# Attention inside a hybrid decoder step: values stationary, probabilities moving, and a new order of the units

## The chip, the cores and the metric

The kernel runs as one program on 1 core of one Trainium2 chip. The metric is device time in microseconds (us); lower is better. The engines are named as in the profile: PE (TensorE, matmuls; PEld its weight loads), DVE (VectorE), ACT (ScalarE), POOL (GpSimd) and SP (SyncE, which here only issues loads). Each engine takes its own instructions strictly in order; engines wait for each other through semaphores.

## The reference, cut to what matters

One layer over 2048 prompt tokens (and 32 sample tokens), width 1024: RMSNorm, one input projection into queries, keys, values and two recurrent branches; windowed attention (8 heads of 64, 2 key/value groups of 4 heads, window 128, with sinks and ALiBi); a gated linear recurrence (RG-LRU) beside it; an output projection with residual; a SwiGLU feed-forward with residual; a final norm.

```
# attention, per 128-query block qb, keys are block qb-1 and block qb
s = q @ k.T / 8 - slope * dist            # masked outside the window
p = exp(s - m);  p = p / (sum(p) + exp(sink - m))
out = p @ v                                # 8 heads x 64
# recurrence, per channel
a = exp(-8 r softplus(-lam));  h = a * h + sqrt(1 - a*a) * (i * x)
mix = concat([out, h * gelu(gate)]);  h1 = x + mix @ w_out + b_out
```

## The kernel before

Tokens go through in 4 blocks of 512; `Fori` runs the first three, the fourth is written out after it, because it also carries the 32 sample tokens (its products are split in two halves of 272 columns). All products are float32 made of three products with rounded high and low parts (`x_hi*w_hi`, `x_lo*w_hi`, `x_hi*w_lo`; L533 to L535), 24 matmuls of 512 columns for a 128-wide output unit. Weight units stream in: SP loads a raw unit (2 buffers), ACT writes its high part (L883), DVE its low part (L1157), PE consumes it (3 buffers).

A block has four stages: head (keys, values, queries), mixers, output projection, feed-forward. The change touches the mixers and the first output units. The mixers run eight units s = 0..7. Each unit has one projection product of a recurrent branch (`gemm`, order x0 x1 y0 x2 y1 x3 y2 y3) and a half of one 128-query attention block (4 heads): `scores(s)` on PE (L628), `softmax_1(s)` on DVE (L1253 to L1264), `exps(s)` on ACT (L961, L963), `softmax_2(s)` on DVE (sum and reciprocal, `rec`), `probs_T(s)` on PE (8 transposes, L644) with its two copies out of PSUM to `pT`, one on ACT (L968, `pTa_ready`) and one on DVE (L1277, `pTb_ready`), and `attend(s)` on PE (L661), which waits for both copies. Probabilities are not normalised; after two units DVE multiplies the 128x512 result by the reciprocals (`attn_out`, L1284), PE transposes it (`attn_T`, L670), ACT copies it and writes its high part (L998, L1001) and DVE its low part (`attn_lo`, L1345), for the output projection.

Between these the same engines carry the recurrence: `conv` (L1290 to L1297) and `evacuate` of the projection (L1170) on DVE, `gates` on PE (L677) at odd s, activations on ACT, `lru_square` (L1319, L1320), `lru_lo` (L1340), `lru_scan` (L1325, L1326, L1328), `lru_mix` (L1334, L1335) and `gelu_arg` (L1312, L1313) on DVE, `lru_root` on ACT (L986, with a table load). The order is written out by hand as three loops over s, one per engine; nothing else sets it. After unit 7, PE starts the first output units in parts (`part`), around the last attention pieces.

Semaphores that matter: `freed(u)` says that DVE has evacuated projection u; `sc_read(s)` that `softmax_1(s)` is done; `p_ready(s)` that `exps(s)` is done.

## Time and profile before

| what | value |
| --- | --- |
| median of 3 runs | 2332.38 us (2332.24 to 2334.09) |
| span of the profiled execution | 2331.0 us |
| granted clock of PE, mean of the span | 0.985 |
| PE busy | 2251.5 us, 97% |
| DVE busy | 1302.4 us, 56% |
| ACT busy | 878.1 us, 38% |

The page gives the profiled execution as its span, first to last instruction; no separate outer time is shown for it. The span lies 1.4 us under the median of the runs. Busy shares are means over stages with different limits: most of the time is projection and feed-forward products, back to back. How the mixers run, which take roughly a sixth of the time, has to be read from the timelines of that stage. In a timeline, a row is a group of like instructions; "[0.97 <-ACT a_tok L998]" is idle time before it and what ended that. In the rows, block 1 is the second of the four, and its units begin at about 622 us.

### The profile page before, as it was taken

What the parts mean: (1) busy time and instruction counts of PE and PEld (TensorE: products, weight loads), DVE (VectorE), ACT (ScalarE), POOL (GpSimd) and SP (SyncE); (2) the same over time, 40 slices, a digit from 0 to 9 for tenths busy, and PEclk for the clock granted to TensorE, in tenths of its full rate; (3) what the DMA queues carried; (4) which work ended last, traced back from release to release, by engine and by line L of the source; (5) the groups of instructions that cost most, each with busy time, mean ns of one, the idle gap of its engine ahead of it and who ended that gap; (6) DMA issues with size and microseconds to landing.
All of it is one profiled execution on the core that took longest, in us unless ns stands there. A gap on an engine that the chain in (4) does not pass through costs nothing.

```text
span 2331.0 us, 31209 instructions
## 1 busy us (share of the span) xinstructions
PE 2251.5 (97%) x12165; PEld 1915.8 (82%) x12165; DVE 1302.4 (56%) x2146; ACT 878.1 (38%) x1349; POOL 32.4 (1%) x66
## 2 busy tenths in 40 slices
PE   6999999999999999999999999999999899999996
PEld 6777888888777888888877788888888799999996
DVE  4786535356587544445668653545668665444453
ACT  4574223235375322223457432323446532222221
POOL 1000000000000000000000000000000000000000
PEclk9999999999999999999999999999999899999998
DMA  4123232323313233332322323233231122222221
GB/s 148 55 68 114 91 100 90 101 89 92 101 46 118 91 97 93 92 98 92 107 67 63 119 91 98 91 97 94 92 124 45 30 91 86 87 91 82 92 80 60
DMA packets 58586, 207.34 MB, mean 89 GB/s; under 512 B 7341, under 2 KB 7549, under 8 KB 58416
## 3 DMA queue, kind: packets, MB, share of 16 engines
q1 hardware_dynamic: 51840, 184.57, 25.5%
q0 software_dynamic: 3936, 12.03, 1.5%
q10 hardware_dynamic: 2656, 8.62, 1.0%
q8 instruction: 104, 1.70, 0.3%
q14 instruction: 50, 0.41, 0.1%
HBM read 196.44 MB, written 9.77 MB: 88 GB/s over the span
## 4 chain that ended last, share of the span: by engine, by line
PE 84%; DVE 9%; ACT 4%; issue 2%; DMA 1%; ACTq 0%; DVEq 0%; POOL 0%
PE bank L533 27%; PE bank L535 27%; PE bank L534 27%; DVE s_p L1258 2%; DVE w_lo L1157 1%; DVE xc L1297 1%; PE bank L661 1%; ACT s_p L961 1%; DVE om L1326 1%; PE bank L628 1%; DVE pT L1277 1%; PE bank L583 1%; ACT L986 0%; PE bank L557 0%; DVE ii L1325 0%
## 5 line engine op out<-in xcount | busy, mean ns | idle before, releaser
L533 PE MATMUL bank<-x_hi,w_hi 128*128 128x512 f32 (+1 forms) x2320 | 826.4, 356 | 3.7 <-DVE x_lo L1187 2.6
L535 PE MATMUL bank<-x_hi,w_lo 128*128 128x512 f32 (+1 forms) x2320 | 820.3, 354 | 0.0
L534 PE MATMUL bank<-x_lo,w_hi 128*128 128x512 f32 (+1 forms) x2320 | 819.5, 353 | 0.0
L883 ACT ACTIVATE w_hi<-w_raw 128x1024 fp32r<-128x1024 f32 (+1 forms) x360 | 374.1, 1040 | 1175.3 <-PE bank L535 1175.3
L533 PEld LDWEIGHTS bank<-x_hi,w_hi 128*128 128x128 f32 x2320 | 438.9, 189 | 79.8 <-issue 13.6
L1157 DVE TENSOR_TENSOR w_lo<-w_raw,w_hi 128x1024 fp32r<-128x1024 f32 (+1 forms) x360 | 431.8, 1200 | 127.7 <-ACT w_hi L883 125.9
L534 PEld LDWEIGHTS bank<-x_lo,w_hi 128*128 128x128 f32 x2320 | 439.1, 189 | 61.8 <-issue 1.4
L535 PEld LDWEIGHTS bank<-x_hi,w_lo 128*128 128x128 f32 x2320 | 438.3, 189 | 60.8
L533 PE MATMUL bank<-a_hi,w_hi 128*128 128x512 f32 (+1 forms) x1200 | 427.4, 356 | 6.2 <-DVE a_lo L1561 1.8
L535 PE MATMUL bank<-a_hi,w_lo 128*128 128x512 f32 (+1 forms) x1200 | 425.0, 354 | 0.0
L534 PE MATMUL bank<-a_lo,w_hi 128*128 128x512 f32 (+1 forms) x1200 | 424.3, 354 | 0.0
L533 PEld LDWEIGHTS bank<-a_hi,w_hi 128*128 128x128 f32 x1200 | 227.6, 190 | 40.6 <-DVE a_lo L1345 3.2
L535 PEld LDWEIGHTS bank<-a_hi,w_lo 128*128 128x128 f32 x1200 | 227.3, 189 | 31.3
L534 PEld LDWEIGHTS bank<-a_lo,w_hi 128*128 128x128 f32 x1200 | 227.7, 190 | 30.5
L1563 DVE TENSOR_TENSOR hT<-bank,hT 128x512 f32<-128x512 f32 (+1 forms) x120 | 70.9, 591 | 235.5 <-PE bank L535 235.3
L1170 DVE TENSOR_TENSOR a<-bank,rinv 128x512 f32<-128x512 f32 (+1 forms) x110 | 65.1, 591 | 229.4 <-PE bank L535 227.6
L1170 DVE TENSOR_TENSOR gt<-bank,rinv 128x512 f32<-128x512 f32 (+1 forms) x110 | 65.0, 591 | 206.4 <-PE bank L535 206.0
L961 ACT ACTIVATE s_p<-s_p,nm 128x256 f32<-128x256 f32 x128 | 63.6, 498 | 51.5 <-DVE sd L1264 51.5
L661 PE MATMUL bank<-v_tok,pT 128*128 128x64 f32 x512 | 63.2, 278 | 8.3 <-ACT a_tok L998 8.3
L661 PEld LDWEIGHTS bank<-v_tok,pT 128*128 128x128 f32 x512 | 61.9, 197 | 10.8 <-issue 10.4
L1102 ACT ACTIVATE a_hi<-a 128x512 fp32r<-128x512 f32 (+1 forms) x88 | 56.3, 639 | 37.0 <-DVE a L1557 35.0
L1557 DVE SCALAR_TENSOR_TENSOR a<-gt,a 128x512 f32<-128x512 f32 (+1 forms) x88 | 61.7, 701 | 3.0
(240 smaller groups left out, 1475.0 us busy)
## 6 DMA issues: line engine op xcount, KB each, us to landing
w_raw<-in_units SPq DMA_DIRECT2D x296, 512.0 KB, 3.5
w_raw<-in_units SPq DMA_DIRECT2D x64, 448.0 KB, 3.3
x_tok<-in_x_prompt POOLq DMA_DIRECT2D x16, 512.0 KB, 6.1
out_y_p<-y_tok ACTq DMA_DIRECT2D x16, 512.0 KB, 3.0
gfin<-in_g_fin POOLq DMA_DIRECT2D x1, 512.0 KB, 7.1
kc_tok<-in_cache_k POOLq DMA_DIRECT2D x1, 512.0 KB, 6.9
vc_tok<-in_cache_v POOLq DMA_DIRECT2D x1, 512.0 KB, 7.3
out_nk_s<-in_cache_k POOLq DMA_DIRECT2D x1, 496.0 KB, 6.5
```

The costliest lines, as they stand in the source:

```text
L533: nc.tensor.matmul(out, h, hi[:, kt, c0:c1], start=(first and kt == kts[0]), stop=False)
L534: nc.tensor.matmul(out, h, lo[:, kt, c0:c1], start=False, stop=False)
L535: mm = nc.tensor.matmul(out, l, hi[:, kt, c0:c1], start=False, stop=(kt == kt_of[u] - 1))
L661: mm = nc.tensor.matmul(V[:, head * HEAD:(head + 1) * HEAD], pT[:, s % 2, 2 * hh + half, :], v_tok[:, qb + half, g * HEAD:(g + 1) * HEAD], ...
L883: w_hi_ready.by(A(w_hi[:, u % RING, 0:n], w_raw[:, u % RAW, 0:n], ACT.Copy))
L961: A(s_p[:, s % 2, hh, :], s_p[:, s % 2, hh, :], ACT.Exp, bias=nm[:, s % 2, hh:hh + 1], accum_out=rs[:, s % 2, hh:hh + 1])
L1102: act_hi.by(A(a_hi[:, f, 0:w], a32[:, n % 2, 0:w], ACT.Copy))
L1157: w_ready.by(TT(w_lo[:, u % RING, 0:n], w_raw[:, u % RAW, 0:n], w_hi[:, u % RING, 0:n], ALU.subtract))
L1170: return lambda src, c0, c1: TT(dst(c0, c1), src, rinv[:, c0:c1], ALU.mult)
L1258: ins = nc.vector.tensor_tensor_reduce(s_p[:, s % 2, hh, :], S[g][:, jj * 256:(jj + 1) * 256], d[:, :], 2.0 ** -(head + 1), sinks[:, head: ...
L1557: act_f.by(STT(out=a32[:, n % 2, 0:w], in0=gt[:, 0:w], scalar=0.5, in1=a32[:, n % 2, 0:w], op0=ALU.mult, op1=ALU.mult))
L1563: evacuate(b, last, u, lambda src, c0, c1: TT(hT[:, m, c0:c1], src, hT[:, m, c0:c1], ALU.add))
```

## The change

1. `attend`: before, the stationary operand is a 128x128 block of transposed probabilities and 64 columns of values move (8 matmuls, float32 runs each in two passes). Now 64 columns of values are stationary, and the probabilities of two heads (256 columns) move: 4 matmuls, alternating between group 0 (output partitions 0 to 63) and group 1 (64 to 127). The result comes out already transposed.
2. `attn_T` goes. The reciprocals now have to stand in every partition of a head's half: `spread` makes 8 matmuls with a reciprocal column broadcast to 64 columns as the stationary operand and the identity moving. ACT copies that to `a_tok` (`attn_recs`), DVE multiplies the result by it (`attn_out`, same size as before).
3. In that layout, tile c of the mixed vector holds head c of both groups, so the rows of the output weights are permuted: each of the 8 output units of a block is loaded with 5 transfers (one of 256 KB, four of 64 KB with runs of 512 bytes) in place of one of 512 KB. The sample tokens' result is written to the same layout.
4. Order on PE: `probs_T(s-1)` moves from the start of unit s to behind its `gemm`; `scores(s)` comes first, then `attend(s-2)`, `spread`; `gates` moves from behind the `gemm` into its middle. On ACT `probs_T(s-1)` moves behind the work on the evacuated projection, `lru_gates` ahead of it. On DVE the copy `probs_T(s-1)` moves from the start of unit s to behind `evacuate(s)`, and `lru_scan` ahead of `evacuate`. The last pieces after unit 7 are reordered alike.

Vector engine, even unit 4, before. `es`, `rec`: softmax_2; `w_lo`: weight split; `yb`: the evacuation; `ii`, `om`, `h_prev`: the scan; `gl`: gelu_arg; `pT`: the copy.

```order
L1270 TENSOR_TENSOR es<-es,rs 128x4 [waits p_ready]
L1272 RECIPROCAL rec<-es 128x2x2 [waits dve_chain]
L68 REGISTER_ALU [waits dve_chain]
L1157 TENSOR_TENSOR w_lo<-w_raw,w_hi 128x1024 [waits w_hi_ready]
L1170 TENSOR_TENSOR yb<-bank,rinv 128x512 [waits gemm_done]
L1325 TENSOR_TENSOR ii<-ii,qq 128x512 [waits lru_sqrt]
L1326 SCALAR_TENSOR_TENSOR om<-ra,h_prev,ii 128x512 [waits dve_chain]
L1328 COPY h_prev<-om 128x1 [waits dve_chain]
L1312 TENSOR_SCALAR gl<-gl 128x512 [waits gelu_sq,dve_chain]
L1313 SCALAR_TENSOR_TENSOR gl<-yb,vec,gl 128x512 [waits dve_chain]
L1277 COPY pT<-bank 128x512 [waits av_done,pT_done]
```

Here the copy `pT` is that of unit 4, the first instruction of unit 5's list. The same place now:

```order
L1305 TENSOR_TENSOR es<-es,rs 128x4 [waits p_ready]
L1307 RECIPROCAL rec<-es 128x2x2 [waits dve_chain]
L68 REGISTER_ALU [waits rec_ready]
L1192 TENSOR_TENSOR w_lo<-w_raw,w_hi 128x1024 [waits w_hi_ready]
L1358 TENSOR_TENSOR ii<-ii,qq 128x512 [waits lru_sqrt]
L1359 SCALAR_TENSOR_TENSOR om<-ra,h_prev,ii 128x512 [waits dve_chain]
L1361 COPY h_prev<-om 128x1 [waits dve_chain]
L1205 TENSOR_TENSOR yb<-bank,rinv 128x512 [waits gemm_done,dve_chain]
L1313 COPY pT<-bank 128x512 [waits av_done,pT_done]
L1345 TENSOR_SCALAR gl<-gl 128x512 [waits gelu_sq]
L1346 SCALAR_TENSOR_TENSOR gl<-yb,vec,gl 128x512 [waits dve_chain]
```

The scan stands ahead of the evacuation, and the copy `pT`, now that of unit 3, right behind it.

PE, ahead of the product of unit 5, before (L644 probs_T, L661 attend, L628 scores).

```order
L644 MATMUL bank<-ident,s_p 128x128 [waits pTb_ready,pTa_ready,p_ready]
L644 MATMUL bank<-ident,s_p 128x128 x7
L661 MATMUL bank<-v_tok,pT 128x64 [waits pTb_ready,pTa_ready]
L661 MATMUL bank<-v_tok,pT 128x64 x7
L628 MATMUL bank<-kT,qT 128x256 [waits sc_read]
L628 MATMUL bank<-kT,qT 128x256 x3
```

The same place now (L660 probs_T, L642 scores, L678 attend, L692 spread).

```order
L660 MATMUL bank<-ident,s_p 128x128 [waits pTb_ready,pTa_ready,p_ready]
L660 MATMUL bank<-ident,s_p 128x128 x7
L68 REGISTER_ALU
L642 MATMUL bank<-kT,qT 128x256 [waits sc_read]
L642 MATMUL bank<-kT,qT 128x256 x3
L678 MATMUL bank<-pT,v_tok 64x256 [waits pTb_ready,pTa_ready]
L678 MATMUL bank<-pT,v_tok 64x256 x3
L692 MATMUL bank<-ident,rec 64x128 [waits rec_ready]
L692 MATMUL bank<-ident,rec 64x128 x7
```

Before, the piece runs from `probs_T(4)` to `scores(5)`, and its attend is `attend(3)`. Now the transposes are `probs_T(3)`, behind the product of unit 4, and the attend is `attend(3)` too, of the copies that these very transposes are read into.

```diff
+                raw, src, landed = w_raw[:, u % RAW, :], units[u % NU], raw_in[u % RAW]
+                if u % NU not in U_O:
+                    landed.by(sp.dma_start(raw[:, 0:n], src[:, 0:n]))
+                    return
+
+                landed.by(sp.dma_start(raw[:, JT * P:n], src[:, JT * P:n]))
+                for g in range(NKV):
+                    for c in range(2):
+                        k = 2 * g + c
+                        landed.by(sp.dma_start(
+                            raw[g * HEAD:(g + 1) * HEAD, 2 * c * P:2 * (c + 1) * P].rearrange("d (o m) -> d o m", o=2),
+                            src[:, k * P:(k + 1) * P].rearrange("(o d) m -> d o m", o=2)))
...
-                        attn_moved.wait(pe, b, qb)
-                    for hh in range(HH):
-                        g, jj = hh // 2, hh % 2
-                        head = g * JT + 2 * jp + jj
-                        for half in range(2):
-                            mm = nc.tensor.matmul(V[:, head * HEAD:(head + 1) * HEAD],
-                                                  pT[:, s % 2, 2 * hh + half, :],
-                                                  v_tok[:, qb + half, g * HEAD:(g + 1) * HEAD],
-                                                  start=(half == 0), stop=(half == 1))
+                        atok_ready.wait(pe, b, qb)
+                    for half in range(2):
+                        for g in range(NKV):
+                            d = slice(g * HEAD, (g + 1) * HEAD)
+                            mm = nc.tensor.matmul(V[d, 2 * jp * P:2 * (jp + 1) * P], v_tok[:, qb + half, d],
+                                                  pT[:, s % 2, 4 * g + half:4 * g + half + 3:2, :],
+                                                  start=(half == 0), stop=(half == 1), skip_group_check=True)
                     av_done.by(mm)
 
-                def attn_T(qb):
-                    atok_ready.wait(pe, b, qb + 1)
-                    for c in range(4):
-                        mm = nc.tensor.transpose(V[:, c * P:(c + 1) * P], a_tok[:, c * P:(c + 1) * P], ident[:, :])
-                    attnT_done.by(mm)
+                def spread(qb):
+
+
+                    rec_ready.wait(pe, b, 2 * qb + 2)
+                    if last and qb == QB - 2:
+                        pe.wait_ge(smp_dve, SMP_DVE_AT)
+                    for j in range(JT):
+                        for g in range(NKV):
+                            head = g * JT + j
+                            mm = nc.tensor.matmul(TB[0][g * HEAD:(g + 1) * HEAD, j * P:(j + 1) * P],
+                                                  rec[:, qb % 2, head:head + 1].to_broadcast([P, HEAD]), ident[:, :],
+                                                  start=True, stop=True, skip_group_check=True)
+                    recs_done.by(mm)
...
+                def attn_recs(qb):
+                    recs_done.wait(act, b, qb + 1)
+                    amix_ready.wait(act, b, qb)
+                    recs_read.by(A(a_tok[:, :], TB[0][:, :], ACT.Copy))
+
                 def attn_hi(qb):
-                    attnT_done.wait(act, b, qb + 1)
-                    attn_moved.by(A(a_tok[:, :], V[:, :], ACT.Copy))
-
-                    attn_moved.wait(act, b, qb + 1)
+                    atok_ready.wait(act, b, qb + 1)
...
                 def attn_out(qb):
-                    av_done.wait(dve, b, 2 * qb + 2)
-                    amix_ready.wait(dve, b, qb)
-                    bc = rec[:, qb % 2, :].rearrange("p (h o) -> p h o", o=1).to_broadcast([P, NH, HEAD])
-                    atok_ready.by(TT(a_tok[:, :].rearrange("p (h d) -> p h d", h=NH),
-                                     V[:, :].rearrange("p (h d) -> p h d", h=NH), bc, ALU.mult))
+                    recs_read.wait(dve, b, qb + 1)
+                    atok_ready.by(TT(a_tok[:, :], V[:, :], a_tok[:, :], ALU.mult))
...
+                    scores(s)
+                    if s >= 2:
+                        attend(s - 2)
+                    if s >= 3 and s % 2 == 1:
+                        spread((s - 3) // 2)
+                    if last:
+                        gemm(b, last, UH + s, x_hi, x_lo, None, None, 0)
+                    else:
+                        gemm(b, last, UH + s, x_hi, x_lo, None, list(range(KT // 2)))
+                    if s % 2 == 1:
+                        gates(s // 2)
+                    if last:
+                        gemm(b, last, UH + s, x_hi, x_lo, None, None, 1)
+                    else:
+                        gemm(b, last, UH + s, x_hi, x_lo, None, list(range(KT // 2, KT)))
                     if s >= 1:
                         probs_T(s - 1)
-                    if s >= 2:
-                        attend(s - 2)
-                    scores(s)
-                    gemm(b, last, UH + s, x_hi, x_lo)
                     if last:
                         for step in sample_at.get(s, ()):
                             step(b, s)
-                    if s % 2 == 1:
-                        gates(s // 2)
-                    if s >= 3 and s % 2 == 1:
-                        attn_T((s - 3) // 2)
...
+                part(0, early)
+                attend(NUN - 2)
                 probs_T(NUN - 1)
-                attend(NUN - 2)
-                part(0, early)
+                part(1, early)
                 attend(NUN - 1)
-                part(1, early)
-                attn_T(QB - 1)
+                spread(QB - 1)
...
                 for s in range(NUN):
-                    if s >= 1:
-                        probs_T(s - 1)
+                    if s >= 3 and s % 2 == 1:
+                        attn_recs((s - 3) // 2)
                     exps(s)
                     if s >= 2 and s % 2 == 0:
                         lru_root((s - 2) // 2)
+                    if s >= 3 and s % 2 == 1:
+                        attn_hi((s - 3) // 2)
+                    if s % 2 == 1:
+                        lru_gates(s // 2)
                     kind, c = ORDER[s]
                     u = UH + s
                     freed.wait(act, b, u + 1)
...
 
                         lmix_ready.wait(act, b, c - 1)
                         gelu_sq.by(A(gl[:, c % 2, :], yb[:, c % 2, 0:T], ACT.Square, bias=v(VB + u)))
-                        if c < LC - 1:
-                            gelu_tanh(c)
-                    if s >= 3 and s % 2 == 1:
-                        attn_hi((s - 3) // 2)
-                    if s % 2 == 1:
-                        lru_gates(s // 2)
+                    if s >= 1:
+                        probs_T(s - 1)
+                    if kind == "y" and c < LC - 1:
+                        gelu_tanh(c)
...
                 for s in range(NUN):
-                    if s >= 1:
-                        probs_T(s - 1)
                     softmax_1(s)
+                    if s >= 3 and s % 2 == 1:
+                        attn_out((s - 3) // 2)
                     if s >= 2 and s % 2 == 0:
                         lru_square((s - 2) // 2)
                     if s >= 4 and s % 2 == 0:
...
                         sample_conv()
                     if last and s == 7:
                         sample_square()
-                    if s >= 3 and s % 2 == 1:
-                        attn_out((s - 3) // 2)
                     if s >= 1:
                         split(b, UH + s - 1 + RING)
                     if s >= 3 and s % 2 == 1:
                         lru_mix((s - 3) // 2)
+                    if s >= 2 and s % 2 == 0:
+                        lru_scan((s - 2) // 2)
                     kind, c = ORDER[s]
                     if kind == "x":
                         evacuate(b, last, UH + s, scaled(
                             lambda c0, c1: xb[:, c % 2, CONV_W - 1 + c0:CONV_W - 1 + c1]))
                     else:
                         evacuate(b, last, UH + s, scaled(lambda c0, c1: yb[:, c % 2, c0:c1]))
+                    if s >= 1:
+                        probs_T(s - 1)
                     if last and s in sample_at:
                         sample_at[s]()
                     if s >= 3 and s % 2 == 1:
                         attn_lo((s - 3) // 2)
                     if kind == "x":
                         conv(c)
-                    if s == NUN - 1:
-                        probs_T(s)
-                    if s >= 2 and s % 2 == 0:
-                        lru_scan((s - 2) // 2)
```

## Rows read from the trace of the kernel before

**Rows 1.** Timeline of PE, units 5 and 6 of block 1; columns: start us, us, what.

```profile
676.74 1.09 PE L644 MATMUL bank<-ident,s_p 128*128 128x128 f32 x8 [0.57 <-ACT es L963]
677.67 1.90 PE L661 MATMUL bank<-v_tok,pT 128*128 128x64 f32 x16
679.49 1.14 PE L628 MATMUL bank<-kT,qT 64*128 64x256 f32 x8
680.56 0.50 PE L533 MATMUL bank<-x_hi,w_hi 128*128 128x512 f32 x1
...
686.24 1.88 PE L677 MATMUL bank<-xc,gates_w 128*128 128x512 f32 x4
687.96 0.60 PE L670 MATMUL bank<-ident,a_tok 128*128 128x128 f32 x4
688.40 1.04 PE L644 MATMUL bank<-ident,s_p 128*128 128x128 f32 x8
690.40 1.97 PE L661 MATMUL bank<-v_tok,pT 128*128 128x64 f32 x16 [0.97 <-ACT a_tok L998]
```

**Rows 2.** Timeline of DVE over units 4 and 5 of the same block.

```profile
671.62 0.68 DVE L1277 COPY pT<-bank 128x512 f32<-128x512 f32 x1
...
674.42 0.69 DVE L1319 SCALAR_TENSOR_TENSOR ii<-ii,xc 128x512 f32<-128x512 f32 x1
...
676.23 0.16 DVE L1270 TENSOR_TENSOR es<-es,rs 128x4 f32<-128x4 f32 x1
...
676.72 1.23 DVE L1157 TENSOR_TENSOR w_lo<-w_raw,w_hi 128x1024 fp32r<-128x1024 f32 x1
677.86 0.68 DVE L1170 TENSOR_TENSOR yb<-bank,rinv 128x512 f32<-128x512 f32 x1
678.66 0.69 DVE L1325 TENSOR_TENSOR ii<-ii,qq 128x512 f32<-128x512 f32 x1
...
680.89 0.43 DVE L1312 TENSOR_SCALAR gl<-gl 128x512 f32<-128x512 f32 x1
...
682.02 0.68 DVE L1277 COPY pT<-bank 128x512 f32<-128x512 f32 x1
...
688.33 0.68 DVE L1170 TENSOR_TENSOR xb<-bank,rinv 128x512 f32<-128x512 f32 x1
690.95 0.69 DVE L1345 TENSOR_TENSOR a_lo<-a_tok,a_hi 128x512 fp32r<-128x512 f32 x1 [1.94 <-ACT a_hi L1001]
...
694.66 0.68 DVE L1277 COPY pT<-bank 128x512 f32<-128x512 f32 x1
```

**Rows 3.** Timeline of ACT in unit 4 of the same block.

```profile
674.51 0.51 ACT L961 ACTIVATE s_p<-s_p,nm 128x256 f32<-128x256 f32 x1 [1.16 <-DVE sd L1264]
...
676.70 1.28 ACT L986 ACT_TABLE_LOAD   x1
...
678.58 0.72 ACT L1019 ACTIVATE gl<-yb,vec 128x512 f32<-128x512 f32 x1
```

**Rows 4.** Timeline of PE, first unit of the same block.

```profile
625.92 2.08 PE L628 MATMUL bank<-kT,qT 64*128 64x256 f32 x6 [3.67 <-issue]
627.92 0.79 PE L533 MATMUL bank<-x_hi,w_hi 128*128 128x512 f32 x1
...
634.76 1.04 PE L644 MATMUL bank<-ident,s_p 128*128 128x128 f32 x8
```

**Rows 5.** One stretch around it: busy us and instructions by engine, PEclk, DMA.

```profile
623.70:630.53 6.83, 4.61 (x12) 3.29 (x12) 2.10 (x11) 1.42 (x2) 0.00 (x0) 0.50 0.18 69
```

**Rows 6.** Timeline of PE, sample attention of the last block.

```profile
1811.21 1.10 PE L786 MATMUL bank<-pcT,vc_tok 128*64 128x16 f32 x16
```

**Rows 7.** DMA issues of the page: KB each, median us to landing.

```profile
w_raw<-in_units SPq DMA_DIRECT2D x296, 512.0 KB, 3.5
...
x_tok<-in_x_prompt POOLq DMA_DIRECT2D x16, 512.0 KB, 6.1
...
kc_tok<-in_cache_k POOLq DMA_DIRECT2D x1, 512.0 KB, 6.9
```

More of the change, by code:

```diff
@@ L282, in sem @@
             return ctx.enter_context(nc.semaphore(name))
-        raw_in = [Signal(sem(f"raw_in{i}"), NU // RAW, 16) for i in range(RAW)]
+        transfers = [1 + NKV * 2 if u in U_O else 1 for u in range(NU)]
+        raw_count = [sum(transfers[u % RAW:u + 1:RAW]) for u in range(NU)]
+        raw_in = [Signal(sem(f"raw_in{i}"), sum(transfers[i::RAW]), 16) for i in range(RAW)]
         w_hi_ready = Signal(sem("w_hi_ready"), NU)
@@ L500, in smp_by, with gemm @@
                 ins.then_inc(smp_pe, 1)
-            def gemm(b, wide, u, hi, lo, tile_ready=None, kts=None, only=None):
-                whole = list(range(kt_of[u]))
-                kts = kts or whole
-                first = kts[0] == (KT - LC if kts != whole else 0)
+            def gemm(b, wide, u, hi, lo, tile_ready=None, kts=None, only=None, begins=0):
+                kts = kts or list(range(kt_of[u]))
+                first = kts[0] == begins
                 final = kts[-1] == kt_of[u] - 1
@@ L879, in split @@
                     return
-                raw_in[u % RAW].wait(act, b, u // RAW + 1)
+                raw_in[u % RAW].wait(act, b, raw_count[u % NU] + u // NU * sum(transfers[u % RAW::RAW]))
                 unit_done(act, b, u - RING)
@@ L1040, in mixers @@
                 lru_hi(LC - 2)
+                attn_recs(QB - 1)
                 lru_decay(LC - 1)
@@ L1370, in mixers @@
                         lru_mix((s - 3) // 2)
+                    if s >= 2 and s % 2 == 0:
+                        lru_scan((s - 2) // 2)
                     kind, c = ORDER[s]
@@ L1391, in mixers @@
                 softmax_2(NUN - 1)
+                probs_T(NUN - 1)
                 lru_lo(LC - 2)
```

23 lines of the change are left out of this document (12 added, 11 removed).

## The prediction

> **What bounds the kernel now.** I read the page first: PE is busy nearly all the span, so what PE does less would seem to be won, and where PE waits it would be lost. Then the timelines of the mixers, the only stage the change touches at length, engine by engine, over a pair of units (an even y unit and an odd x unit), since the pattern repeats by pairs. The reader is to see there that PE is not what sets the pace. From one copy `pT` of unit 3 to that of unit 5, two units later, DVE takes 694.66 - 671.62 = 23.04 us [rows 2], and in that time it waits once for long, 1.94 us, for ACT's `a_hi`. PE waits twice in a pair, 0.57 us for the exponentials and 0.97 us for `a_tok` [rows 1]. So both engines are within two microseconds of full, DVE is the one whose list closes the loop, and PE is let go by it. What decides the change is therefore how tightly the two lists hang together, more than the length of either.
>
> **PE's work, part by part.** `attend` takes 679.49 - 677.67 = 1.82 us for 16 passes, `probs_T` 0.93, `scores` 680.56 - 679.49 = 1.07, a product 686.24 - 680.56 = 5.68, `gates` 687.96 - 686.24 = 1.72, `attn_T` 0.44 [rows 1]. `gates` is 4 passes of 512 columns, so a pass costs 0.43 us per 512 columns, 0.21 per 256, 0.11 per 128. The new `attend` has 8 passes of 256 columns, the new `spread` 16 of 128: each 1.72 us if the passes run one after the other, 0.86 if the two groups run at the same time. No row has two matmuls side by side in column halves. The nearest is `scores`: it too has 8 passes of 256 columns, in two row halves of 64, and takes 1.07 where one after the other would be 1.72; the two halves run together, with 0.21 left for the passage between shapes. The sample's attention has 64-column weights, 16 passes in 1.03 to 1.10 us [rows 6], 0.07 each, so loading such weights doesn't bound either. I take 1.05 for `attend` and 0.95 for `spread`; the other end is 1.8 and 1.8. A pair of units then has 2 x 1.05 + 0.95 = 3.0 us where it had 2 x 1.82 + 0.44 = 4.1: 1.1 us less (or 1.3 more).
>
> The Trainium skill (TensorEngine Tiling, Key Properties) says that different tiles of the array load and multiply in parallel, and that a change of tiling mode drains the engine. By it the side-by-side value holds; the drains are the 0.21 us in `scores`, and the trace agrees as far as row halves show it. No run here shows column halves yet.
>
> **The new loop.** DVE's work stays as it was: the multiplication has the same size. Its order doesn't. Before, the copies of `probs_T(s-1)` stood at the start of DVE's unit s, so `attend` found them made long ago. Now `attend(s-2)` in PE's unit s needs the copies of `probs_T(s-2)`, which DVE makes in unit s-1 behind `evacuate(s-1)`, and the product of unit s stands behind that `attend`. So PE can't start a product before DVE has evacuated the last one and copied, and DVE can't evacuate before the product is done. They alternate. Follow a pair, from DVE's start of the evacuation of an odd unit.
>
> DVE's half: 0.9 until PE's transposes are complete; copy and `softmax_1` 674.42 - 671.62 = 2.80; between them `attn_lo` and `conv` 694.66 - 690.95 = 3.71 (the 1.94 wait is gone, since `a_hi` is now made earlier). From the end of `softmax_1` the scan waits for ACT: exponentials 676.70 - 674.51 = 2.19, then table load and root, together 678.66 - 674.42 = 4.24 [rows 2, 3]. DVE's own work in that time (`lru_square`, `lru_lo`, `softmax_2` and the split) is over at 677.86 - 674.42 = 3.44, so 0.8 is waited; before, the evacuation filled it. The scan is 680.89 - 678.66 = 2.23, then the evacuation 0.69. The copy on DVE would take 0.68, but ACT's half of it now stands behind `gelu_sq`, 0.66 + 0.58 (`gelu_sq` is 0.72 with some overlap; the size of ACT's copy I take a little under DVE's), and 0.15 of hops: 1.4. Sum 0.9 + 2.8 + 3.7 + 4.24 + 2.23 + 0.69 + 1.4 = 15.9 us. PE, meanwhile, does transposes, scores, attend, product, transposes and scores, 0.9 + 1.07 + 1.05 + 5.68 + 0.93 + 1.07 = 10.7, and then stands 5.2 us in front of `attend` of the odd unit.
>
> PE's half: attend 1.05, `spread` 0.95, product 5.68, `gates` 1.72, end of the pipeline and hop 0.2: 9.6 us. DVE has 688.33 - 682.02 = 6.3 us of work in that time and then waits about 2.6 for the product.
>
> A pair is 15.9 + 9.6 = 25.5 us against 23.04: 2.4 slower, although PE has less to do. Three pairs in a block (the loop closes at units 2, 4 and 6 into 3, 5 and 7): 7.3.
>
> At the ends of the stage. `gates(0)` now stands in the middle of product 1 and waits for `softmax_1(1)`, which DVE does behind evacuation, ACT's bias and `conv`: 0.69 + 0.72 + 3.1 + 2.2, about 6.9 with hops after product 0, where PE is there after scores and half a product, 1.07 + 2.84 = 3.9. It waits 3.0, of which less `attend` work and the rest of the product behind it give some back: +1.3. Behind unit 7, `spread(3)`, ACT's copy, ACT's decay and tanh (four instructions of the size of its 0.72, which stand before `a_hi`; about 2.8 us), `a_hi` and `a_lo` are a chain of about 6 us behind `attend(7)`, covered by 1.4 us of the third output unit and what PE does itself; PE waits some 3.5 before the late parts, nearly all of it new: +3.5. Per block 7.3 + 1.3 + 3.5 = 12, three blocks 36. In the last block a product is longer (two halves of 272 columns), which was on the path before as after, and the sample steps now stand behind `probs_T` and three of them wait for its copies: 12 + 4 = 16. Sum so far: 52.
>
> **The clock.** PE stood 3.67 us before block 1's first scores, and then 6 passes of `scores` took 2.0 us (627.92 - 625.92) where 6 of 8 passes are 0.8, and the product took 634.76 - 627.92 = 6.84 where it is 5.68 [rows 1, 4]: 2.4 us lost. In that stretch the granted clock was 0.50, that is 1.2 in place of 2.4 GHz [rows 5]; PE had been idle before it fell. The new order has five stands of over 3 us in a block (three of 5.2, the `gates` one, the last one), each followed by work that lies on the path. At 2.4 each that would be 12 a block; at nothing, 0. A part of a low stretch may lie inside the stand itself, and shorter stands do not always bring it, so I take 7: 28 us over four blocks.
>
> **Costs taken at nothing.** The five transfers for an output unit: a raw buffer is free from one split to the next but one, two products of 5.68 us less the two splits (twice the 1.14 of [rows 2]), 9 us, and a unit lands in 3.5; 512 KB in runs of 512 bytes (`kc_tok`) landed in 6.9 where whole rows of 4 KB (`x_tok`) took 6.1 [rows 7], both on POOL's queue. So I expect under 6 us, covered; uncovered it would cost 32 units times the excess, per two units. DVE's multiplication and ACT's copy are as big as before. The rearranged sample copies are as many.
>
> **Sum.** 2331.0 + 52 + 28 = 2411 for the profiled span; the median of runs stands 1.4 above the span, so about 2412.
>
> **Rivals.**
> - The same loop, but PE's clock stays up after the stands: 2331 + 52 + 1.4 = 2384 us. For it: no stand in the mixers of 5 us exists in the trace to judge by. Against: the row at 0.50.
> - The column halves don't run together: `attend` 1.8 and `spread` 1.8 add 1.6 to PE's half of each pair and some 2 at the tail, 7 a block, so 2412 + 28 = 2440. For it: no row with column halves. Against: `scores`.
> - The five transfers are slow: if each took 3.5 us one after another, 17.5 + 2.3 = 19.8 us for two units in place of 11.4, 4.2 us a unit, 32 units: about 2412 + 134 = 2546. Against it: the 512-byte row.
> - Faster: the loop doesn't close, because `attend` finds its copies early. Then PE's two waits go, and DVE's 1.94, and a pair is 23.04 - 1.9 = 21.1 us, DVE's bare work; 12 pairs give 23 us, 2309. It decides where DVE's half is shorter than PE's way to `attend`, 10.7; I find 15.9, so 5 us of error in one place would be needed. For it: PE truly has 1.1 us less per pair, and both waits of [rows 1] truly go.
> - The gains and the loop cancel: within 0.2%.
>
> **Chances.** Forecast 0.52; clock stays up 0.17; one after the other 0.18; transfers 0.03; faster 0.07; cancels 0.03. Within 0.2% (4.7 us) is what a measurement here can't tell from no change. Faster by more 0.07, same 0.03, slower 0.90. The likeliest is 2412. The range goes from 2365, below the clock case because the last block and the ends are worked out loosely, to 2450, above the serial one.
>
> **What would show it.** Right: on PE, idle of 4 to 6 us before `attend` in units 3, 5 and 7, released by a `pT` copy of ACT; on DVE a wait for the product of 2 to 3 us at the odd evacuations; a pair of 25 to 28 us; no wait on `a_tok`; `attend` 1.0 to 1.1 us and `spread` about 0.95; PEclk of 0.5 in several stretches of each mixers stage; product times in feed-forward and head unchanged. Wrong: `attend` without idle before it, or the pair at 21 us (the loop as I drew it isn't there); `attend` at 1.8 (no side by side); idle before output products ended by a load.

## The result, and the profile after

| | before | after |
| --- | --- | --- |
| median, us (4 runs each, same chip) | 2332.31 (2331.34 to 2334.09) | 2408.41 (2406.77 to 2409.41) |
| ratio, 95% interval | | 1.0324 [1.0309, 1.0339] |
| span of the profiled execution, us | 2331.0 | 2407.7 |
| mean granted clock of PE | 0.985 | 0.967 |

Slower by 76 us; 2412 was predicted. On the page PE has more busy time than before, although its matmuls in the mixers became shorter, and its share fell from 97% to 94%. A low clock makes busy time longer, so that number alone would mislead.

```profile
PE 2261.5 (94%) x12101; PEld 1897.0 (79%) x12101; DVE 1305.6 (54%) x2146; ACT 878.9 (37%) x1349; POOL 32.5 (1%) x66
```

The timeline of PE after, block 1, its gates(0), units 3 to 7 and the first late parts (start us, us, what). It answers to [rows 1, 4].

```profile
657.82 3.78 PE L701 MATMUL bank<-xc,gates_w 128*128 128x512 f32 x4 [2.92 <-DVE sd L1299]
...
665.22 1.04 PE L660 MATMUL bank<-ident,s_p 128*128 128x128 f32 x8
...
680.86 1.97 PE L678 MATMUL bank<-pT,v_tok 128*64 128x256 f32 x8 [4.65 <-ACT pT L998]
...
693.90 1.08 PE L678 MATMUL bank<-pT,v_tok 128*64 128x256 f32 x8
...
700.58 1.03 PE L660 MATMUL bank<-ident,s_p 128*128 128x128 f32 x8
...
707.75 1.98 PE L678 MATMUL bank<-pT,v_tok 128*64 128x256 f32 x8 [5.06 <-ACT pT L998]
709.51 1.92 PE L692 MATMUL bank<-ident,rec 128*64 128x128 f32 x16
...
714.28 1.88 PE L701 MATMUL bank<-xc,gates_w 128*128 128x512 f32 x4
...
734.80 1.97 PE L678 MATMUL bank<-pT,v_tok 128*64 128x256 f32 x8 [5.05 <-ACT pT L998]
...
754.41 0.50 PE L547 MATMUL bank<-a_hi,w_hi 128*128 128x512 f32 x1 [0.74 <-DVE w_lo L1192]
...
758.52 0.50 PE L547 MATMUL bank<-a_hi,w_hi 128*128 128x512 f32 x1 [1.75 <-DVE a_lo L1378]
```

To read there: PE stands 4.65 to 5.06 us in front of `attend` (L678) of the odd units, and what ends the stand is ACT's copy `pT`. In the even units (693.90) it doesn't stand at all. A pair of units, from odd `attend` to odd `attend`, takes 707.75 - 680.86 = 26.89 and 734.80 - 707.75 = 27.05 us, where it had 23.04 [rows 2]. Right behind a stand `attend` is busy for 1.98 us, elsewhere for 1.08.

The other side of the loop, in the timeline of DVE after; it answers to [rows 2].

```profile
703.53 0.69 DVE L1358 TENSOR_TENSOR ii<-ii,qq 128x512 f32<-128x512 f32 x1 [0.71 <-ACT qq L1016]
...
705.76 0.69 DVE L1205 TENSOR_TENSOR yb<-bank,rinv 128x512 f32<-128x512 f32 x1
...
718.97 0.69 DVE L1205 TENSOR_TENSOR xb<-bank,rinv 128x512 f32<-128x512 f32 x1 [3.15 <-PE bank L549]
```

And of ACT, which makes the other half of the copy.

```profile
706.49 0.72 ACT L1055 ACTIVATE gl<-yb,vec 128x512 f32<-128x512 f32 x1 [2.99 <-DVE yb L1205]
707.12 0.58 ACT L998 ACTIVATE pT<-bank 128x512 f32<-128x512 f32 x1
```

The product that `yb` evacuates ended about where the transposes behind it begin, at 700.58, but DVE comes to it at 705.76: the scan, which waits for ACT's root `qq`, stands ahead. Only then come evacuation, `gelu_sq`, ACT's copy (ends 707.70) and `attend` (707.75). In the other half DVE waits 3.15 us for PE. The engines take turns.

The stage by windows, block 1 from its first scores to its first late part, one stretch around a stand, and one in the last block (stretch, length, busy us and instructions of PE, PEld, DVE, ACT and POOL, PEclk, DMA). First before:

```profile
625.92:722.54 96.62, 92.77 (x500) 72.79 (x499) 77.09 (x194) 67.19 (x142) 0.00 (x0) 0.98 0.14 45
```

Then after:

```profile
641.73:758.52 116.79, 96.39 (x484) 69.07 (x483) 78.07 (x194) 68.62 (x142) 0.00 (x0) 0.88 0.12 36
704.60:711.40 6.80, 3.65 (x25) 2.56 (x25) 5.62 (x17) 4.07 (x5) 0.00 (x0) 0.50 0.17 52
1885.60:1906.10 20.50, 14.32 (x85) 11.67 (x86) 7.68 (x28) 8.16 (x22) 0.00 (x0) 0.50 0.09 27
```

The stage is 116.79 - 96.62 = 20.2 us longer. Its idle time went from 3.9 to 20.4 us. From 704.60 to 711.40, around a stand, the granted clock was 0.50, that is 1.2 GHz; PE had been idle before. The last stretch belongs to the last block and is read below.

Where in the block the 20.2 lie is read against three rows of PE in before:

```profile
655.06 1.90 PE L661 MATMUL bank<-v_tok,pT 128*128 128x64 f32 x16
...
700.70 1.90 PE L661 MATMUL bank<-v_tok,pT 128*128 128x64 f32 x16
...
1729.86 1.14 PE L628 MATMUL bank<-kT,qT 64*128 64x256 f32 x8 [1.42 <-ACT qT L948]
```

Up to the `attend` of unit 3: 680.86 - 641.73 = 39.1 against 655.06 - 625.92 = 29.1, +10.0 (the stand of gates(0) and the first stand before `attend`). The next two pairs: 53.94 against 45.64, +8.3. From there to the late part: 23.7 against 21.8, +1.9. Over the program: block 1 begins 641.73 - 625.92 = 15.8 later, the scores of the last block 1786.00 - 1729.86 = 56.1 later (row below), so blocks 1 and 2 together cost 40.3; the last one and what follows cost 76.7 - 56.1 = 20.6.

The last block shows that the same total can come from other places. PE after:

```profile
1786.00 1.14 PE L642 MATMUL bank<-kT,qT 64*128 64x256 f32 x8 [1.41 <-ACT qT L978]
...
1826.85 1.97 PE L678 MATMUL bank<-pT,v_tok 128*64 128x256 f32 x8 [4.68 <-ACT pT L998]
...
1857.47 1.97 PE L678 MATMUL bank<-pT,v_tok 128*64 128x256 f32 x8
...
1889.75 1.86 PE L816 MATMUL bank<-pcT,vc_tok 128*64 128x16 f32 x16 [8.71 <-ACT pT L998]
...
1902.25 1.97 PE L678 MATMUL bank<-pT,v_tok 128*64 128x256 f32 x8
```

Here only unit 3 has the stand before `attend`. In units 5 and 7 (1857.47 and 1902.25) PE waits ahead of the scores instead, 2.89 and 2.03 us, both for sample work, and `attend` behind them still takes 1.97 us. The sample attention (L816) waits 8.71 us for an ACT copy, and from 1885.60 to 1906.10, 20.5 us on end, the granted clock is 0.50 (the window above).

### The profile page after: what moved, and what is told of

It is laid out like the page before. It is cut to its first block, busy times and chain, and to the rows that moved or that the text cites. A ratio compares the mean times of both kernels' runs of the same rounds, so it can differ in the third digit from the quotient of the medians.

```text
span 2407.7 us, 31226 instructions
## 1 busy us (share of the span) xinstructions
PE 2261.5 (94%) x12101; PEld 1897.0 (79%) x12101; DVE 1305.6 (54%) x2146; ACT 878.9 (37%) x1349; POOL 32.5 (1%) x66
## 4 chain that ended last, share of the span: by engine, by line
PE 86%; DVE 7%; ACT 4%; issue 2%; DMA 1%; ACTq 0%; POOL 0%; DVEq 0%
PE bank L547 26%; PE bank L549 26%; PE bank L548 26%; PE bank L701 1%; PE bank L678 1%; DVE s_p L1293 1%; DVE xc L1330 1%; PE bank L692 1%; ACT s_p L991 1%; DVE om L1359 1%; ACT L1016 1%; PE bank L660 1%; PE bank L597 1%; PE bank L571 0%; PE bank L642 0%
## 5 line engine op out<-in xcount | busy, mean ns | idle before, releaser
L547 PE MATMUL bank<-x_hi,w_hi 128*128 128x512 f32 (+1 forms) x2320 | 834.8, 360 | 3.1 <-DVE x_lo L1222 1.9
L678 PE MATMUL bank<-pT,v_tok 128*64 128x256 f32 x256 | 45.4, 487 | 52.0 <-ACT pT L998 49.0
L678 PEld LDWEIGHTS bank<-pT,v_tok 128*64 128x64 f32 x256 | 19.1, 166 | 71.9 <-ACT pT L998 60.2
```

The lines of the kernel that those rows point to most:

```text
L547: nc.tensor.matmul(out, h, hi[:, kt, c0:c1], start=(first and kt == kts[0]), stop=False)
L678: mm = nc.tensor.matmul(V[d, 2 * jp * P:2 * (jp + 1) * P], v_tok[:, qb + half, d], pT[:, s % 2, 4 * g + half:4 * g + half + 3:2, :], start ...
```

## The experiments

Each edit is to the changed kernel, unless it says otherwise. Times are medians; each ratio is against the kernel before, run on the same chip.

**e1_scan_back** moves one call on DVE, the scan, back behind the evacuation and the copy.

```diff
-                    if s >= 2 and s % 2 == 0:
-                        lru_scan((s - 2) // 2)
                     kind, c = ORDER[s]
...
                     if kind == "x":
                         conv(c)
+                    if s >= 2 and s % 2 == 0:
+                        lru_scan((s - 2) // 2)
```

> The changed kernel with one part undone: DVE's scan stands behind the evacuation and the copy of the probabilities again, as before the change. Theory A (DVE and PE alternate, and DVE's half is lengthened by the scan's wait for ACT's root and by the scan): the way from the end of softmax_1 to the even evacuation falls from 4.24 + 2.23 us to 3.44, so PE's stand before attend of the odd units falls from 5 us to about 2, and a pair of units from 27.0 us to 22.5 (24 if the clock still falls behind the stand). Twelve pairs: 2408 - 36 to - 54, so 2354 to 2372 us. Rival B (the stands come from PE's own new work or from the output units' transfers): no change, 2408.

Measured 2365.7 us (2364.89 to 2367.79), ratio 1.0146 [1.0129, 1.0163]: 43 of the 76 us are back by one call. PE in its timeline:

```profile
647.11 3.78 PE L701 MATMUL bank<-xc,gates_w 128*128 128x512 f32 x4 [2.92 <-DVE sd L1299]
...
689.26 1.08 PE L678 MATMUL bank<-pT,v_tok 128*64 128x256 f32 x8 [2.00 <-ACT pT L998]
690.17 1.04 PE L692 MATMUL bank<-ident,rec 128*64 128x128 f32 x16
...
711.73 1.08 PE L678 MATMUL bank<-pT,v_tok 128*64 128x256 f32 x8 [2.00 <-ACT pT L998]
```

The pair is 711.73 - 689.26 = 22.47 us, the stand 2.00 in place of 5.06, and `attend` is 1.08 behind it: the clock did not fall there. The gates(0) stand of 2.92 with its slow 3.78 is unchanged. So the pairs hang on what stands between the product's end and DVE's evacuation.

**e2_copy_first** puts ACT's copy ahead of its work on the evacuated product (`gelu_sq` or the bias).

```diff
                         lru_gates(s // 2)
+                    if s >= 1:
+                        probs_T(s - 1)
                     kind, c = ORDER[s]
...
-                    if s >= 1:
-                        probs_T(s - 1)
                     if kind == "y" and c < LC - 1:
```

> The changed kernel with ACT's copy of the probabilities ahead of its work on the evacuated projection (in an even unit ahead of gelu_sq). Theory A: ACT's copy is what ends PE's stand; with it early DVE's own copy ends it, 0.6 us sooner in each odd unit, 12 times: about 2401 us, and the stand is released by DVE. Rival B (another wait sets the pair): within 0.1% of 2408.

Measured 2406.97 us (2406.47 to 2408.83), ratio 1.0323 [1.0306, 1.0340]: no gain, against the expectation.

```profile
708.49 1.98 PE L678 MATMUL bank<-pT,v_tok 128*64 128x256 f32 x8 [4.69 <-DVE pT L1313]
...
735.71 1.97 PE L678 MATMUL bank<-pT,v_tok 128*64 128x256 f32 x8 [4.69 <-DVE pT L1313]
```

The stand is 0.37 us shorter and DVE's copy now ends it, as expected, but the pair is 735.71 - 708.49 = 27.22 us, not shorter. A window around the first of these rows shows where the gain went:

```profile
706.90:713.70 6.80, 5.21 (x28) 3.99 (x29) 5.46 (x19) 5.07 (x10) 0.00 (x0) 0.50 0.10 27
```

The stretch at 0.50 is as long here as in after (704.60 to 711.40 above), but it begins 1.6 us before `attend` and not 3.2. So PE works 5.21 us of it at the low clock, where after works 3.65. From `attend` to `gates` it then takes 715.70 - 708.49 = 7.21 us, where after takes 714.28 - 707.75 = 6.53. Why the stretch begins later in the stand isn't shown.

**e3_filled** has PE work in its stand: 18 (in the last block 30 narrower) matmuls whose result is thrown away.

```diff
                 for s in range(NUN):
                     scores(s)
+                    if s >= 3 and s % 2 == 1:
+                        fill(s, 18 if not last else 30)
                     if s >= 2:
```

> The changed kernel with added work: ahead of attend in units 3, 5 and 7 PE runs 18 more matmuls of 512 columns (30 of 272 in the last block) into the bank that the next product overwrites; nobody reads them. They take 4.2 us of a stand of 5. Theory A (the clock falls because PE stands, and costs 1.4 us in each pair): the granted clock stays at 1.0 behind the filled stands, attend takes 1.0 us instead of 1.8, a pair 25.6 instead of 27.0, and the kernel gets faster by about 17 us, 2391, though it does more. Rival B (attend, spread and the first product are slow behind a stand for a reason other than the clock, or the added work delays attend): 2408 or more.

Measured 2396.02 us (2393.22 to 2398.39), ratio 1.0269 [1.0252, 1.0287]: 12 us faster with more work. PE's rows:

```profile
701.08 1.08 PE L678 MATMUL bank<-pT,v_tok 128*64 128x256 f32 x8 [0.72 <-ACT pT L1013]
...
705.87 1.88 PE L701 MATMUL bank<-xc,gates_w 128*128 128x512 f32 x4
...
726.39 1.08 PE L678 MATMUL bank<-pT,v_tok 128*64 128x256 f32 x8 [0.72 <-ACT pT L1013]
...
1769.24 1.14 PE L642 MATMUL bank<-kT,qT 64*128 64x256 f32 x8 [1.41 <-ACT qT L993]
...
1839.19 5.09 PE L715 MATMUL bank<-x_hi,w_hi 128*128 128x272 f32 x30
1844.21 1.08 PE L678 MATMUL bank<-pT,v_tok 128*64 128x256 f32 x8
```

and the stage of block 1, from first scores to first late part as before:

```profile
637.22:748.26 111.04, 103.65 (x537) 75.19 (x537) 78.05 (x194) 68.06 (x142) 0.00 (x0) 0.96 0.13 39
```

The loop still takes turns, but at 2.4 GHz (0.96 over the stage, where after has 0.88): the pair is 726.39 - 701.08 = 25.31 us. From `attend` to `gates` it takes 705.87 - 701.08 = 4.79 us, where after takes 6.53. So one such stand costs 1.74 us through the clock, beside its own length. The gain fell short of the 17 expected in one place: the scores of the last block come 1786.00 - 1769.24 = 16.8 us earlier, and then 5.7 are lost again (the two profiled executions differ by 11.1). Two of the three odd units of that block, 5 and 7, have no stand before `attend` to fill. There the added work lies on the path: 1844.21 - 1839.19 = 5.0 us in unit 5, as much in unit 7, of which the clock gives back some 2 each.

**e4_one_transfer** loads each output unit in one transfer.

```diff
-        transfers = [1 + NKV * 2 if u in U_O else 1 for u in range(NU)]
+        transfers = [1 for u in range(NU)]
...
-                if u % NU not in U_O:
+                if True:
                     landed.by(sp.dma_start(raw[:, 0:n], src[:, 0:n]))
```

> The changed kernel with each output unit loaded by one transfer of 512 KB as before the change; the rows of the output weights are then left in the old order, so the output projection multiplies the wrong heads. Theory A (the five transfers are covered): within 0.1% of 2408. Rival B (a wait for the splits of an output unit is longer for them; one of 0.74 us stands ahead of the third output unit): faster by up to 4 x 0.7 = 3 us or more.

Measured 2408.0 us (2406.21 to 2410.21), ratio 1.0322 [1.0305, 1.0339]: the five transfers cost nothing that can be measured.

**e5_scan_gates_back** is e1 and, besides, `gates` behind the whole product on PE, with ACT's part behind the bias.

```diff
                         gemm(b, last, UH + s, x_hi, x_lo, None, list(range(KT // 2)))
-                    if s % 2 == 1:
-                        gates(s // 2)
...
                         gemm(b, last, UH + s, x_hi, x_lo, None, list(range(KT // 2, KT)))
+                    if s % 2 == 1:
+                        gates(s // 2)
```

> Two parts of the order undone: the scan behind the evacuation (as in e1_scan_back, 2366 us) and the gates' matmuls behind the whole product again, with ACT's gates behind the bias. Theory A (in the middle of product 1 they wait 2.9 us for softmax_1(1) and drag the clock down behind it; elsewhere their place is indifferent, because the copies of the probabilities wait for the transposes behind both): no stand at gates(0), no low clock there, the other pairs stay at 22.5 us; 3 us a block, about 2354 us. Rival B (the middle place hides gates and is a gain in the later units): slower than 2366.

Measured 2350.47 us (2347.3 to 2352.47), ratio 1.0076 [1.0060, 1.0093]: 15 us less than e1, 3.8 a block. The place of `gates` (on PE, with ACT's part) was the second cost. `gates(0)` starts at 642.46 without idle before it, and from the first scores of block 1 to the `attend` of unit 3 it takes 657.41 - 625.63 = 31.8 us, where e1 takes 667.02 - 630.73 = 36.3. Part of these 4.5 us is lost again, for the expectation missed something: PE now waits some 2 us before the scores of even units. PE, unit 4 of block 1, and the same unit one block later:

```profile
669.72 1.14 PE L642 MATMUL bank<-kT,qT 64*128 64x256 f32 x8 [1.98 <-ACT ii L1005]
670.79 1.08 PE L678 MATMUL bank<-pT,v_tok 128*64 128x256 f32 x8
...
1225.42 1.53 PE L642 MATMUL bank<-kT,qT 64*128 64x256 f32 x8 [1.98 <-ACT ii L1005]
1226.88 1.97 PE L678 MATMUL bank<-pT,v_tok 128*64 128x256 f32 x8
```

The same wait of 1.98 us has the full clock behind it once and the low one the other time. Where the clock stays up a pair takes 679.70 - 657.41 = 22.3 us; in the next block, where it falls, 1236.94 - 1213.12 = 23.8.

**e6_old_order** keeps the new matmuls and gives all three engines the old order, as far as the new operations allow.

```diff
                 for s in range(NUN):
+                    if s >= 1:
+                        probs_T(s - 1)
                     scores(s)
                     if s >= 2:
                         attend(s - 2)
-                    if s >= 3 and s % 2 == 1:
-                        spread((s - 3) // 2)
...
-                    if s % 2 == 1:
-                        gates(s // 2)
+                    if s >= 3 and s % 2 == 1:
+                        spread((s - 3) // 2)
...
-                    if s >= 1:
-                        probs_T(s - 1)
...
+                    if s % 2 == 1:
+                        gates(s // 2)
```

DVE and ACT likewise: `probs_T(s - 1)` at the start of the unit, `lru_scan` behind the evacuation.

> The new matmuls in the old order: attend with values stationary, spread and the five transfers of the changed kernel, but transposes and copies of the probabilities at the start of a unit as before, gates behind the product, the scan behind the evacuation; spread stands in the middle of the odd products, ACT copies its result ahead of the bias, DVE multiplies behind the evacuation and writes a_lo behind conv. Theory A (all of the loss is the order; the new matmuls themselves save PE 1.1 us a pair and take a_tok's copy off attend's path): PE waits under 1 us anywhere, a pair 22 us against 23.04 of the kernel before, about 3 us a block: 2319 us (2312 to 2326). Rival B (DVE's list alone bounds the stage, so the matmuls are worth nothing): 2331. Rival C (the new matmuls or transfers cost): over 2335.

Measured 2324.36 us (2321.26 to 2324.69), ratio 0.9963 [0.9949, 0.9977]: faster than before. Run again as e10 it gave 2322.54 and 0.9964 [0.9950, 0.9977]. PE:

```profile
663.57 1.14 PE L642 MATMUL bank<-kT,qT 64*128 64x256 f32 x8 [0.76 <-ACT ii L1007]
664.64 1.08 PE L678 MATMUL bank<-pT,v_tok 128*64 128x256 f32 x8
...
678.17 1.09 PE L693 MATMUL bank<-ident,rec 128*64 128x128 f32 x16 [0.74 <-ACT pT L1000]
...
686.68 1.08 PE L678 MATMUL bank<-pT,v_tok 128*64 128x256 f32 x8
```

The pair is 686.68 - 664.64 = 22.04 us, 1.0 below before, as the 1.1 us less work on PE would have it (the two waits of a pair, 0.76 and 0.74, add up to what the 0.57 and 0.97 of before did). `attend` waits for nothing; two waits of about 0.75 us remain, at the scores of the even unit and at `spread` (L693), which stands in the middle of the product and needs the bank that ACT's copy frees.

**e7_group_by_group** issues the four matmuls of `attend` in the order group 0, 0, 1, 1 in place of 0, 1, 0, 1.

```diff
-                    for half in range(2):
-                        for g in range(NKV):
+                    for g in range(NKV):
+                        for half in range(2):
```

> The changed kernel with attend's four matmuls issued group by group (0, 0, 1, 1) in place of alternating. Theory A (the two column halves run at the same time as the row halves of scores do, which are issued group by group): attend stays at 1.0 to 1.1 us, 2408. Rival B (only neighbours in the list overlap): attend takes 1.3 to 1.8 us, a pair up to 0.8 us longer in its PE half, up to 2418.

Measured 2407.75 us (2405.64 to 2408.99), ratio 1.0324 [1.0307, 1.0342]. The row for all of L678 in this kernel, minimum, median and maximum of one pass in ns:

```profile
L678 PE MATMUL bank<-pT,v_tok x256: 379/430/689, 95.2 to 1917.5; 128*64 128x256 f32 x128
```

After has 379/430/688: no difference. That two passes run side by side, and not merely fast, is seen in the starts of the single passes, which the timeline gathers into one row. In e1's `attend` at 689.26 the eight begin at 689.261 and 689.267, 689.527 and 689.534, 689.743 and 689.750, 689.959 and 689.966; in e7 the two of a pair are 13 to 14 ns apart. That it takes both halves shows in the sample attention of before, whose 64-column weights all lie in one half (`TB[g][0:HEAD]`): there no two of a group's 16 passes begin together; after the first they follow each other by 58 to 59 ns.

So with four passes of a group in a row (e7) the halves still overlap. With many in a row they don't, as far as row halves show it. The sample scores of after issue 16 passes of one group (and two of another matmul) before the other group's:

```profile
L793 PE MATMUL bank<-kc_T,q_d x32: 272/272/373, 1848.7 to 1852.1; 64*128 64x128 f32 x32
```

32 passes of 128 columns in 3.4 us are 0.11 each, one after the other; only where the groups meet do two begin together (1850.367 and 1850.373). For long runs of one group the order of issue may well matter; no run tests it for column halves.

**e8_scan_back_copy_first** is e1 and e2 at once: is e2's edit worth something when the clock stays up?

```diff
+                    if s >= 1:
+                        probs_T(s - 1)
                     kind, c = ORDER[s]
...
+                    if s >= 2 and s % 2 == 0:
+                        lru_scan((s - 2) // 2)
```

> e1_scan_back (2366 us) with ACT's copy ahead of its other work too. Theory A (in e2_copy_first the stand got 0.4 us shorter, but spread and product behind it lost as much to the low clock; behind the 2 us stands of e1_scan_back the clock does not fall, so here the same edit is worth what it takes off): a pair 22.0 instead of 22.5, 12 times: about 2360 us. Rival B (the edit is worth nothing in itself): 2366.

Measured 2360.25 us (2356.89 to 2364.89), ratio 1.0116 [1.0099, 1.0132], against 1.0146 [1.0129, 1.0163] for e1: the intervals touch, so a gain of some 5 us is likely and not shown. PE:

```profile
687.71 1.08 PE L678 MATMUL bank<-pT,v_tok 128*64 128x256 f32 x8 [1.66 <-DVE pT L1313]
...
693.14 1.98 PE L701 MATMUL bank<-xc,gates_w 128*128 128x512 f32 x4 [0.49 <-DVE sd L1299]
...
710.23 1.08 PE L678 MATMUL bank<-pT,v_tok 128*64 128x256 f32 x8 [1.65 <-DVE pT L1313]
```

The stand is 0.34 us shorter than in e1, but the pair, 710.23 - 687.71 = 22.52, is not: `gates` then waits 0.49 us for `softmax_1` on DVE. The time came near the number expected of the theory that the edit helps when the clock stays up; the mechanism did not show, at least in the profiled execution (2364.89, the slowest of the four). The pair is set by DVE's list there, not by ACT's copy.

**e9_spread_late** is e6 with its two remaining waits attacked: `spread` behind 6 of the 8 parts of the product, and in even units `attend` ahead of `scores`.

The diff is to e6.

```diff
+                    if s >= 2 and s % 2 == 0:
+                        attend(s - 2)
                     scores(s)
-                    if s >= 2:
+                    if s >= 3 and s % 2 == 1:
                         attend(s - 2)
...
-                        gemm(b, last, UH + s, x_hi, x_lo, None, list(range(KT // 2)))
+                        gemm(b, last, UH + s, x_hi, x_lo, None, list(range(KT - 2)))
                     if s >= 3 and s % 2 == 1:
                         spread((s - 3) // 2)
```

> e6_old_order with two places changed on PE, except in the last block for the first: spread stands behind six of the eight parts of the odd product instead of four (there it waited 0.7 us for ACT's copy of the probabilities), and in even units attend stands ahead of scores (which waited 0.8 us for ACT's gates). Theory A (PE's two waits set part of the pair): both waits vanish, a pair 22.0 to 21.4 us, 9 to 12 pairs, 6 us: 2318. Rival B (DVE's list sets the pair at 22.0): PE waits elsewhere, 2324 again.

Measured 2313.28 us (2312.52 to 2316.82), ratio 0.9926 [0.9912, 0.9940], beside 0.9964 for e10, run on the same chip. It is the fastest version. PE:

```profile
660.59 1.08 PE L678 MATMUL bank<-pT,v_tok 128*64 128x256 f32 x8
662.17 1.14 PE L642 MATMUL bank<-kT,qT 64*128 64x256 f32 x8 [0.50 <-ACT ii L1009]
...
676.77 1.09 PE L693 MATMUL bank<-ident,rec 128*64 128x128 f32 x16
...
681.97 1.08 PE L678 MATMUL bank<-pT,v_tok 128*64 128x256 f32 x8
```

`spread` waits no longer, the scores wait 0.50, and the pair is 681.97 - 660.59 = 21.38 us. Only PE's order differs from e6 here, so the rival that DVE's list sets the pair at 22.0 falls.

**e10_old_order_again** is e6 once more, unchanged, to see that its small gain stands.

> e6_old_order once more, beside e9_spread_late on the same chip and in more rounds. If the gain over the kernel before is real: ratio 0.9965 within 0.0015, about 2324 us. If it was the chip's scatter: the interval holds 1.

It does: 2322.54 us (2321.28 to 2325.34).

## Why the prediction was right

The step that decided held: the two lists alternate. Point by point.

- **What set the pace before.** The prediction took it that DVE's list closes the loop and lets PE go. e6 and e9 don't bear that out as it stands. With less work on PE the pair fell from 23.04 to 22.04 us (e6), and with PE's order alone changed to 21.38 (e9), so PE's list had a part in the 23.04. The forecast of the change didn't rest on this.
- **The loop.** Predicted: PE's half, DVE's half, a pair of 25.5 us without the clock. With the clock kept up (e3) it is 25.31. DVE's half, from the odd evacuation to the end of ACT's copy, was worked out as 15.9 and is 15.8 (734.80 - 718.97, from the evacuation to the `attend` that it lets go). The stand before `attend` was to be 5.2 and is 4.65 to 5.06, ended by the ACT copy named; DVE's wait at the odd evacuation was put at 2.6 (9.6 less 6.3, the prediction's own terms, would be 3.3), and it is 3.15. That the scan's place is the cause, and not the matmuls, e1 shows: 43 us for one call.
- **The new matmuls.** `attend` was taken at 1.05 and occupies PE 709.51 - 707.75 = 1.76 us at the low clock and 690.17 - 689.26 = 0.91 at the high one (e1). One after the other it would be 1.72 at the high one. The rival in which the groups run in turn falls, by this and by the starts of the single passes (e7). That the matmuls are worth something is shown by e6 and e9, which have them and beat before by 8 and 18 us; e9's part of that is also its own order.
- **gates(0).** The stand was to be 3.0 and is 2.92. What it costs was put too low: 1.3, with a share of the clock. Taking it away (e5 against e1) gives 3.8 a block, net of the new waits that e5 has. From 657.82 to 665.22 PE needs 7.40 us for `gates` and half a product, where 1.72 and 2.84 would be 4.56 at the high clock [rows 1]: 2.84 lie in the clock.
- **The tail.** PE was to wait 3.5 before the late parts. It waits 0.74 and 1.75, and from the last odd `attend` on the stage is 1.9 us longer: the term was about 1.6 too high.
- **The clock.** 7 a block was taken, between 0 and 12. Three stands at 1.74 and gates(0) at 2.84 are 8.1 in block 1. The rival in which the clock stays up falls by the window at 0.50 and by e3. That shorter stands don't always bring the low clock, as the prediction has it, e1 and e5 bear out.
- **The transfers.** Nothing was taken, and e4 shows nothing.
- **The blocks.** 12 + 7 = 19 were predicted for a looped block and 23 for the last; measured 15.8 up to the start of block 1, then 40.3 for two blocks, and 20.6. In the last block the total was right by luck, for the loop that it was mostly made of is there once: one stand before `attend` and not three, and in place of the others waits of 2.89 and 2.03 us before scores, a wait of 8.71 us at the sample attention and 20.5 us at the low clock around it. The prediction had named only that the sample steps would wait for the copies.

So errors of both signs cancel within each block: gates(0) with its clock was sized too low, the tail too high. The closeness of 2408 to 2412 is better than the single terms deserve.

What the parts of the change are worth, in the order in which they were undone: the scan's place 43 us (e1), that of `gates` 15 (e5), those of the transposes, copies, `spread` and the last pieces 26 together (e6); what is left is 8 faster than before. The 26 are not split further.

Open: whether the copy order on ACT is worth the 5 us that e8 hints at (e8's and e1's profiled executions have the same span, 2363.2 us); why the low clock begins later in the stand in e2; and why the same wait of 1.98 us brings it once and once not in e5.

## What to carry to other kernels

Where two engines that take their work in order hand buffers to each other in every unit, keep a unit of slack between a copy and its consumer; "behind the next product" sounds like hiding, but it put the consumer in front of the product that the copying engine itself waits for. Trace the cycle through all lists before counting what an engine saves: here 1.1 us less per pair on PE became 2.3 more through the loop and 1.7 through the clock. And when an arrangement is slower, test the new operations under the old order before dropping both: they were worth keeping.

## What the runs showed of the hardware

- Two matmuls with 64-column weights in the two column halves run at the same time: 8 passes of 256 columns in 0.91 us, where one after the other they would need 1.72, alternating or four passes of a group at a time (e7). Their starts lie 6 to 14 ns apart in pairs. Passes that all use one half follow one another (sample attention of before, sample scores of after). The Trainium skill (TensorEngine Tiling (Array Packing), Key Properties) says that tiles work independently; the trace agrees. Its other sentence there is that a change of mode drains the engine. The 0.91 can't show that, since it stands behind an idle PE and ahead of `spread`, which has the same mode. Where `attend` stands between scores and a product it takes 665.66 - 664.64 = 1.02 us (e6), about 0.1 more, so a drain, if that is what it is, costs little here.
- Around a stand of 5.06 us the granted clock was 0.50 in after, and behind all three stands of 4.65 to 5.06 us in block 1 `attend` took 1.97 to 1.98 us. Behind one of 2.00 (e1) it took its full-clock 1.08. But the length of the last stand alone doesn't decide: behind 1.98 us it took 1.08 in one block and 1.97 in the next (e5). The cost of a stand can then be more than its length, 1.74 us more in the mixers, and throwaway work in it made the kernel 12 us faster (e3).
- A shorter stand needn't give its time back: in e2 more of an equally long stretch at 0.50 fell on work.
- Loads of 64 KB in 512-byte runs landed in 2.4 us, beside 3.5 for 512 KB, as the page of after has them (medians from issue to landing, 128 and 264 loads).
